# RWKV decay products: DVE evicts one of four matrices, ACT copies three, GpSimd masks them in SBUF

## The reference

```python
def wkv_scan(s0, r, decay, k, v, kk, a):
    def step(s, inp):
        r_t, w_t, k_t, v_t, kk_t, a_t = inp
        sa = jnp.einsum("bhij,bhj->bhi", s, -kk_t)
        s = (s * w_t[:, :, None, :] + sa[..., None] * (kk_t * a_t)[:, :, None, :]
             + v_t[..., None] * k_t[:, :, None, :])
        return s, jnp.einsum("bhij,bhj->bhi", s, r_t)
    xs = tuple(jnp.moveaxis(z, 1, 0) for z in (r, decay, k, v, kk, a))
    s, o = lax.scan(step, s0, xs)
    return s, jnp.moveaxis(o, 0, 1)
```

## Time and profile before

| | us |
|---|---|
| median of 3 timed runs | 2350.82 |
| the three runs | 2348.98 to 2351.67 |
| the profiled execution, its own time | 2344.9 |
| its span in the trace | 2343.3 |
| busy: PE | 2159.1 (92%) |
| busy: PEld | 1416.1 (60%) |
| busy: DVE | 911.4 (39%) |
| busy: ACT | 634.3 (27%) |
| busy: POOL | 319.2 (14%) |
| granted TensorE clock, mean | 0.96 |

### The profile page before, as it was taken

How to read it: one execution, slowest core, us unless ns; L and a number is a source line. 1 busy time by engine, 2 the same in 40 slices (tenths; PEclk the granted TensorE clock), 3 DMA queues, 4 the chain that set the end, 5 groups by cost and what they waited for, 6 DMA issues and landing times. The chain is left out here.

```text
span 2343.3 us, 47109 instructions
## 1 busy us (share of the span) xinstructions
PE 2159.1 (92%) x20794; PEld 1416.1 (60%) x20794; DVE 911.4 (39%) x1765; ACT 634.3 (27%) x1433; POOL 319.2 (14%) x279
## 2 busy tenths in 40 slices
PE   7999999999999999997997999999898788589997
PEld 3577585775866857654554555555566555355664
DVE  3253462543634526323314313053322677522332
ACT  5321222223222223121214111121222566211111
POOL 0000020110201102020001032120010566101110
PEclk9999999999999999999989999999898899699998
DMA  7000010000100000007002021100002000546652
GB/s 254 30 20 11 10 40 19 29 21 10 31 29 29 12 19 30 21 15 280 1 27 104 27 84 65 65 10 9 28 27 72 1 1 1 190 179 226 210 194 92
DMA packets 52798, 147.84 MB, mean 63 GB/s; under 512 B 11459, under 2 KB 20995, under 8 KB 51316
## 3 DMA queue, kind: packets, MB, share of 16 engines
q1 hardware_dynamic: 42612, 103.97, 12.7%
q0 software_dynamic: 9984, 40.87, 4.9%
HBM read 123.58 MB, written 21.24 MB: 62 GB/s over the span
## 5 line engine op out<-in xcount | busy, mean ns | idle before, releaser
L755 PE MATMUL psum<-xT,rw_w 128*128 128x384 f32 (+1 forms) x1152 | 397.7, 484 | 2.8 <-PEq L169 2.8
L755 PEld LDWEIGHTS psum<-xT,rw_w 128*128 128x128 f32 x1152 | 206.1, 189 | 119.9 <-issue 9.4
L2014 PE MATMUL psum<-spare,xT 128*128 128x384 f32 (+1 forms) x432 | 143.3, 494 | 1.5 <-PEq L169 1.5
L2014 PE MATMUL psum<-kvq_w,xT 128*128 128x384 f32 (+1 forms) x432 | 140.6, 487 | 0.0
L1292 DVE SCALAR_TENSOR_TENSOR rwkv_xs<-psum,rwkv_pc,rwkv_xsc 128x64 f32<-128x64 f32 x90 | 25.6, 284 | 238.9 <-PE psum L968 238.9
L2014 PEld LDWEIGHTS psum<-spare,xT 128*128 128x128 f32 (+1 forms) x432 | 80.4, 187 | 62.7 <-issue 13.6
L2014 PEld LDWEIGHTS psum<-kvq_w,xT 128*128 128x128 f32 (+1 forms) x432 | 79.0, 184 | 61.3 <-issue 11.2
L723 POOL DMA_DIRECT2D out<-rwkv_s x6 | 5.7, 953 | 760.5 <-ACT rwkv_out_p L1118 760.5
L1097 ACT COPY rwkv_r_sb<-psum 128x64 f32<-128x64 f32 x96 | 20.4, 212 | 327.9 <-PE psum L948 296.2
L2416 PE MATMUL psum<-V,yT 128*128 128x512 f32 x192 | 105.2, 675 | 0.0
L2093 DVE TENSOR_REDUCE kvq_ss<-kvq_sq 128x6 f32<-128x384 f32 (+1 forms) x36 | 19.9, 552 | 201.8 <-ACT kvq_sq L2056 201.7
(11 more groups left out here) (437 smaller groups left out, 4051.0 us busy)
## 6 DMA issues: line engine op xcount, KB each, us to landing
xT<-in_cache_k SPq DMA_DIRECT2D x64, 384.0 KB, 3.8
samp_vp<-in_cache_v POOLq DMA_DIRECT2D x64, 384.0 KB, 4.5
rw_w<-in_w_in SPq DMA_DIRECT2D x28, 512.0 KB, 3.6
front_w<-in_mem_w_kv SPq DMA_DIRECT2D x2, 2048.0 KB, 14.5
x_rows<-in_x_p SPq DMA_DIRECT2D x8, 512.0 KB, 14.0
h<-in_x_p SPq DMA_DIRECT2D x8, 512.0 KB, 13.3
residual<-h POOLq DMA_DIRECT2D x8, 512.0 KB, 3.3
xT<-in_w_out SPq DMA_DIRECT2D x2, 1536.0 KB, 13.1
```

Of the source, the lines that this page charges most:

```text
L755: mm = pe.matmul(out, w[:, load % 2, k, :], xT[:, k, a:b], start=(k == 0), stop=(k == KC - 1))
L2014: mm = pe.matmul(bank[0:r, j % 6, 0:W], xT[:, k, n * P:n * P + r], w[i % 2][:, k, :], start=(k == 0), stop=(k == KC - 1))
```

## The change

The eviction of a product is divided among three engines. DVE masks and writes only the first of the four matrices (128 columns of a product, 64 of the last), and signals `am_ready` as before. ACT waits for `am_ready`, then copies the other three matrices (384 columns, 192 of the last) from the same bank, without a mask, and signals the new `amc_ready`. GpSimd, in `mask_products`, waits until the copies of a group are there and multiplies them in place by the masks (768 columns a group, 192 for the last), signalling `am_masked`. For pair 0 it does so at once; for the later pairs the masks stand inside `normalize`, between the bias and the wait for the scale. TensorE waits for `amc_ready` before the last product and before each turn, and for all five `am_masked` before `recurrence`. ACT's copies of the turned groups 0 to 2 to `dd` now stand between its new copies.

The first part of the diff, left out here, only adds the two semaphores `amc_ready` and `am_masked` to the list.

```diff
--- before.py
+++ after.py
...
@@ -699,6 +699,14 @@
         def _(pool):
             link = Chain(pool, pool_chain)
 
+            def mask_products(p):
+                for g in range(NG):
+                    a = am[:, group(g), 1:4, :].rearrange("p n a t -> p n (a t)")
+                    n = 4 if g < GROUPS else 1
+                    pool.wait_ge(amc_ready, NFILL * p + min(2 * g + 2, NFILL))
+                    m = const_view(const, "mask4" if g < GROUPS else "mask4s")[:, CH:4 * CH]
+                    nc.gpsimd.tensor_tensor(a, a, bcast(m.unsqueeze(1), [P, n, 3 * CH]), ALU.mult).then_inc(am_masked, 1)
+
             def normalize(p):
                 pool.wait_ge(mean_ready, p + 1)
                 link(nc.gpsimd.tensor_tensor(o_all[:, :, :], o_all[:, :, :], bcast(stat[:, 0, :].unsqueeze(2), [P, NCHUNK, HS]), ALU.subtract))
@@ -706,6 +714,8 @@
                 g = rows[:, p * HS:(p + 1) * HS]
                 bias = rows[:, (PAIRS + p) * HS:(PAIRS + p + 1) * HS]
                 link(nc.gpsimd.tensor_tensor(ov[:, p % 2], ov[:, p % 2], bcast(bias.unsqueeze(1), [P, NCHUNK, HS]), ALU.add))
+                if p + 1 < PAIRS:
+                    mask_products(p + 1)
                 pool.wait_ge(scale_ready, p + 1)
                 link(nc.gpsimd.tensor_tensor(o_all[:, :, :], o_all[:, :, :], bcast(stat[:, 3, :].unsqueeze(2), [P, NCHUNK, HS]), ALU.mult))
                 link(nc.gpsimd.tensor_tensor(o_all[:, :, :], o_all[:, :, :], bcast(g.unsqueeze(1), [P, NCHUNK, HS]), ALU.mult))
@@ -716,7 +726,9 @@
                 pool.dma_start(y_d[:, p, :], gT[p % 2][:, :]).then_inc(y_stored, 16)
 
             for p in range(PAIRS):
-                if p >= 1:
+                if p == 0:
+                    mask_products(0)
+                else:
                     normalize(p - 1)
                     store_y(p - 1)
                 pool.wait_ge(st_ready, 2 * (p + 1))
@@ -800,7 +812,7 @@
                 if f == 7:
                     pe.wait_ge(ov_ready, p + 1)
                 if f == 8:
-                    pe.wait_ge(am_ready, NFILL * p + 1)
+                    pe.wait_ge(amc_ready, NFILL * p + 1)
                 for n in range(2 * f, min(2 * f + 2, NCHUNK)):
                     for i, src in enumerate((beT, kaT)):
                         for d in half:
@@ -811,6 +823,7 @@
 
             def first_inverse(p, g):
                 pe.wait_ge(e0_ready, NG * p + g + 1)
+                pe.wait_ge(amc_ready, NFILL * p + min(2 * g + 2, NFILL))
                 for u in range(4 if g < GROUPS else 1):
                     for d in half:
                         mm = turned(bank[d, g, u * CH:(u + 1) * CH], ee[d, 4 * g + u, :], d)
@@ -938,6 +951,7 @@
                     mm.then_inc(s_turned, 1)
 
             def recurrence(p):
+                pe.wait_ge(am_masked, NG * (p + 1))
                 for n in range(NPC):
                     x = xs[:, n % 2, :]
                     for d in half:
@@ -1084,7 +1098,19 @@
                 act.wait_ge(tok_turned, 7 * (p + 1))
                 nc.scalar.copy(v_tok[:, NPC, :], bank[:, 6, 0:CH])
                 nc.scalar.copy(tok[:, :, NPC, :], bank[:, 6, CH:3 * CH].rearrange("p (c i) -> p c i", c=2)).then_inc(tok_ready, 1)
-                for g in range(NG):
+                for f in range(NFILL):
+                    act.wait_ge(am_ready, NFILL * p + f + 1)
+                    b = (7 + f) % 8
+                    if f < 8:
+                        ins = nc.scalar.copy(am[:, 2 * f:2 * f + 2, 1:4, :].rearrange("p n a t -> p n (a t)"),
+                                             bank[:, b, :].rearrange("p (n c) -> p n c", n=2)[:, :, CH:4 * CH])
+                    else:
+                        ins = nc.scalar.copy(am[:, NPC, 1:4, :].rearrange("p a t -> p (a t)"), bank[:, b, CH:4 * CH])
+                    ins.then_inc(amc_ready, 1)
+                    if f >= 3 and f % 2 == 1:
+                        act.wait_ge(d0_turned, NG * p + f // 2)
+                        nc.scalar.copy(dd[:, group(f // 2 - 1), :], turn_bank(f // 2 - 1, f // 2 - 1)).then_inc(d0_ready, 1)
+                for g in range(GROUPS - 1, NG):
                     act.wait_ge(d0_turned, NG * p + g + 1)
                     nc.scalar.copy(dd[:, group(g), :], turn_bank(g, g)).then_inc(d0_ready, 1)
                 for k, (lev, g) in enumerate(STEPS[:NTURN]):
@@ -1247,12 +1273,10 @@
                     dve.wait_ge(am_mm, NFILL * p + f + 1)
                     b = (7 + f) % 8
                     if f < 8:
-                        ins = nc.vector.tensor_tensor(am[:, 2 * f:2 * f + 2, :, :].rearrange("p n a t -> p n (a t)"),
-                                                      bank[:, b, :].rearrange("p (n c) -> p n c", n=2),
-                                                      bcast(const_view(const, "mask4").unsqueeze(1), [P, 2, 4 * CH]), ALU.mult)
+                        ins = nc.vector.tensor_tensor(am[:, 2 * f:2 * f + 2, 0, :], bank[:, b, :].rearrange("p (n c) -> p n c", n=2)[:, :, 0:CH],
+                                                      bcast(const_view(const, "mask4")[:, 0:CH].unsqueeze(1), [P, 2, CH]), ALU.mult)
                     else:
-                        ins = nc.vector.tensor_tensor(am[:, NPC, :, :].rearrange("p a t -> p (a t)"), bank[:, b, 0:4 * CH],
-                                                      const_view(const, "mask4s"), ALU.mult)
+                        ins = nc.vector.tensor_tensor(am[:, NPC, 0, :], bank[:, b, 0:CH], const_view(const, "mask4s")[:, 0:CH], ALU.mult)
                     ins.then_inc(am_ready, 1)
                     if f == 5:
                         dve.wait_ge(tok_ready, 7 * (p + 1))
```

More of the change, by code:

```diff
@@ L624, in rwkv_pairs @@
         (s0_loaded, hv_ready, piece_done, prev_ready, mix_read, th_read, h_read, g_tanh, gate_read, sq_ready, sig_ready,
-         cum_ready, dec_ready, rn_ln, rn_ready, prep_ready, tok_turned, tok_ready, am_mm, am_ready, ov_ready, e0_ready,
+         cum_ready, dec_ready, rn_ln, rn_ready, prep_ready, tok_turned, tok_ready, am_mm, am_ready, amc_ready, am_masked, ov_ready, e0_ready,
          d0_turned, d0_ready, m_mm, m_ready, dm_mm, d_ready, e_turned, e_ready, fin_ready, r_mm, r_ready, sa_mm, sa_ready,
@@ L630, in rwkv_pairs @@
             "s0_loaded hv_ready piece_done prev_ready mix_read th_read h_read g_tanh gate_read sq_ready sig_ready "
-            "cum_ready dec_ready rn_ln rn_ready prep_ready tok_turned tok_ready am_mm am_ready ov_ready e0_ready "
+            "cum_ready dec_ready rn_ln rn_ready prep_ready tok_turned tok_ready am_mm am_ready amc_ready am_masked ov_ready e0_ready "
             "d0_turned d0_ready m_mm m_ready dm_mm d_ready e_turned e_ready fin_ready r_mm r_ready sa_mm sa_ready "
```

## The result

The changed kernel takes 2363.87 us (median of 5 runs, 2359.9 to 2371.28) against 2348.98 us of the kernel before, measured beside it in 5 runs. The ratio is 1.0078, with a 95% interval from 1.0063 to 1.0093: 18.3 us slower (0.0078 x 2348.98). It is estimated from all the runs and is not the quotient of the two medians, which lie 14.9 us apart. The profiled execution took 2360.14 us, 15.2 us more than the one of before (2344.9). The forecast was +16.6 us and 2367.4 us, with a range from 2353 to 2375.

A forecast was written before the change was run, and what follows sets the result against it. DVE was taken to set the pace in the decay products, stalling TensorE at the turns; masks locking DVE out add 2.76 us a pair, +16.6 in six, on 2350.82: 2367.4 us, range 2353 to 2375.

The forecast's parts named there:

- The sum: First product to last turn of a pair: the last turn (group 4) comes 2.76 us later.
- the walk: Pair 1 step by step, GpSimd's masks and DVE's two-input start operations locking each other out: +2.76 us; chance 0.58.
- The terms: Single operations in a pair: DVE evictions 0.28 us, ACT copies 0.478, GpSimd masks 1.81 and 0.59, 7.8 a pair.
- the prediction's sign: In the profile after, all five GpSimd masks of a pair would have recorded times over 1.81 us.
- What was costed at nothing: Masks' own end and TensorE's wait before the recurrence, some 29 us behind the last mask; ACT's copies hidden by DVE.
- The step from six pairs to the total: Six pairs' shifts add up to +16.6 us, with levels, recurrence and later stages as before.
- Rival 1: DVE keeps the lock between a group's two start operations: +1.4 us a pair, 2359.2 us; chance 0.17.
- Rival 2: No lock between DVE's start operations and GpSimd's masks: -1.36 us a pair, 2342.6 us, faster; chance 0.15.
- Rival 3: Three or four holds more, each group of a pair held twice: at most +4.6 us a pair, 2378.4 us; chance 0.10.

The follow-up runs named there:

- late masks: Changed kernel with GpSimd starting a pair's masks only when DVE has finished the start matrices of all five groups; 2338.85 us, ratio 0.9969.
- no masks: Changed kernel without GpSimd's masks or the wait for them, ACT's copies multiplying by zero instead; ratio 0.9970.
- before, plus masks: Kernel before with GpSimd's masks added at the same places, and the wait for them before the recurrence; ratio 1.0180.
- masks twice: Changed kernel with each GpSimd mask applied twice in a row; ratio 1.0207.
- changed, ov first: Changed kernel, masks in their early places, with DVE's product for ov moved ahead of the first eviction; ratio 1.0049.

## Why the prediction was right

**The sum.** Forecast +2.76 us a pair, measured +2.55. Turn by turn, in the clock of the trace before (5.59 taken off): turn 0 at 458.34 for 458.39 forecast, turn 1 462.09 for 462.08, product 7 463.75 for 463.66, turn 2 465.82 for 465.89, turn 3 467.14 for 467.21, turn 4 469.42 for 469.63. The order in which DVE and POOL took turns was the forecast's in every group, also where the walk left little room: the first mask was issued at 457.88, 0.16 us behind L1265, and group 3 slipped through ahead of the fourth mask. Of the 0.21 us that the sum was too large, 0.07 are there at turn 3. The rest lies in group 4: ACT's copy of product 7 was done at 466.86 and not at 467.04, the fourth mask was issued at 466.94, and L1264 ended at 468.82, not at 468.99.

**The terms.** Evictions 0.283 us (forecast 0.28), copies 0.479 (0.478), masks 1.81 and 0.58 (1.81 and 0.59). Only two of a pair's five masks have recorded times well over 1.81 (1.93 to 2.01), those issued while a start operation ran; the prediction's sign had it of all five. L1264 of group 1, issued 464.59, ended 465.68, which is 460.09 in the clock of before: the forecast to 0.01 us.

**What was costed at nothing** was nothing: TensorE has no stop for ACT's copies, the wait ahead of the recurrence is met some 30 us before (last mask to 474.88, recurrence from 504.9), and late masks and no masks give the same time.

**The step from six pairs to the total** held in the time, but not in all its parts. Six times 2.55 are 15.3 us. The ratio gives 18.3, with an interval from 14.8 to 21.8 that holds 15.3 too, so the timed runs don't show a remainder. The traces show two parts that the prediction left out and that nearly cancel. The last instruction of the RWKV stage ends at 1078.22 us for 1060.13 before, 18.1 us later: the levels did not stay as before, since two pairs lost clock (see the last section). The stages behind it took 1280.3 us for 1283.1, although no line of them was changed; in the traces of all twelve kernels they take 1279.4 to 1286.0. That the profiled execution came out 15.2 us longer, close to six stretches, is therefore partly luck, and so is part of the nearness of the forecast's 16.6.

**The rivals.** Rival 1 (DVE keeps the lock) falls by the order seen in "before, plus masks", and by L1265 of group 1 in the changed kernel itself: it was issued 0.04 us after L1264 and took 1.91 us. Rival 2 (no lock) falls by every trace here; its -1.36 us is what late masks give, at -1.31. Rival 3's holds did not come together, though "masks twice" shows what they cost.

The Trainium skill's page "SBUF — State Buffer", section "Who interferes with whom", calls the shared pair an exclusive lock. The runs agree for GpSimd's two-input operations. For the one-input operation tried here they don't agree that it is held for the whole instruction: 0.8 of 2.13 us.

## What to carry to other kernels

Work moved to GpSimd isn't free because GpSimd is idle: ask which DVE operations with two inputs in SBUF run in that time, and whether they are on the path. If they are, let the GpSimd work wait until they are through, or let DVE read one operand from PSUM; here one wait on GpSimd's queue was worth 1.1%. And when the operations alternate in a chain, count each hold: a GpSimd operation that waits gets in between two DVE operations that are only 0.04 us apart.

## What the runs showed of the hardware

**TensorE's clock after a stretch full of stops.** In the changed kernel the levels of two of the six pairs, the fourth and the last, run at a granted clock of 0.89 over their first 15 us. From last turn to recurrence these two take 32.14 and 32.61 us, where before they took 30.19 and 30.54 at 1.00. A clock of 0.89 over 15 us is worth 0.11 x 15 = 1.7 us by an estimate, most of the 2.0 and 2.1. The rest may be chance: in the kernels that held 1.00 this part of a pair, the first left out, took anything from 29.6 to 31.6 us. The fourth pair in pieces of 5 us (window, length, busy by engine, granted clock):

```profile
620.00:625.00 5.00, 3.73 (x68) 3.03 (x64) 5.00 (x5) 1.14 (x3) 3.39 (x2) 1.00 0.00 0
625.00:630.00 5.00, 2.56 (x65) 2.18 (x67) 4.83 (x10) 2.04 (x6) 2.35 (x2) 1.00 0.01 3
630.00:635.00 5.00, 5.00 (x126) 5.00 (x124) 3.40 (x9) 0.00 (x0) 0.00 (x0) 0.66 0.01 3
635.00:640.00 5.00, 5.00 (x178) 5.00 (x176) 2.81 (x8) 4.06 (x8) 0.00 (x0) 1.00 0.01 3
```

The clock falls to its lower level for part of the third piece, behind two pieces in which PE was busy 3.73 and 2.56 of 5 us. With masks twice it does so in all six pairs, and lower (mean 0.80 to 0.88 over the 15 us). Its second pair:

```profile
323.00:328.00 5.00, 1.12 (x16) 0.93 (x16) 4.90 (x5) 0.69 (x2) 4.84 (x4) 0.68 0.00 0
328.00:333.00 5.00, 3.99 (x74) 3.99 (x76) 3.48 (x6) 0.21 (x1) 2.02 (x3) 0.50 0.00 0
333.00:338.00 5.00, 5.00 (x146) 5.00 (x144) 2.34 (x7) 1.19 (x4) 0.00 (x0) 0.80 0.02 5
```

There the second piece is at 0.50, the 1.2 GHz level throughout. "Before, plus masks" has it in five pairs of six, "changed, ov first" in one; the other eight kernels, the one before among them, in no levels of their profiled executions. Over the six pairs the time from last turn to recurrence is 13.7 us longer than before in "masks twice" and 9.7 us in "before, plus masks"; the same estimate, the missing clock times 15 us, gives 13 and 11. The timed runs show 8.6 and 9.8 us beyond the stretches: 48.6 where 6.66 x 6 = 40.0 stand, and 42 where 5.36 x 6 = 32.2 do. That the stops cause it was not tried by itself, for instance by filling them with other matmuls; the traces only show that the two go together.

**How long a hold lasts** was the whole of POOL's two-input TENSOR_TENSOR, and 0.8 us of its one-input TENSOR_SCALAR. A held operation of 256 columns ends 0.28 us behind the release, where it takes 0.42 alone. A TENSOR_SCALAR of POOL over 768 columns takes 2.13 us, longer than the 1.81 of the TENSOR_TENSOR.
